# A two-layer block on one core: ends of stages by token halves, low parts in place, second layer by projection

## The chip, the core and the metric

The kernel runs on one core of one Trainium2 chip (trn2). The metric is the time of one execution on the device in microseconds (us). The program uses TensorE (PE in the profile, with its weight loads as PEld), VectorE (DVE), ScalarE (ACT), GpSimd (POOL) and SyncE (SP), which issues the loads and stores.

## The reference, cut to what matters

The input x is 256 tokens by 1024 channels in float32, with a context of 256 tokens and a conditioning vector. Two parts follow each other.

```python
# part 1, twice (a0, a1)
shift, scale, gate = split(silu(c) @ w_ada + b_ada)      # one vector of 1024 each
h = rms_norm(x, pre_g) * (1 + scale) + shift
q, k, v, g = split(h @ w_in)                             # two groups of 8 heads, 64 wide
y = concat(attention_a * silu(ga), attention_b * silu(gb)) @ w_out
x = x + gate * rms_norm(y, post_g)
# part 2: m00 (on x and on the context), m01, m02, m10, m11, m12, each of the form
h = rms_norm(x, g) * (1 + scale) + shift
x = x + gate * sublayer(h)     # m00, m02, m10, m12: 0.5 * gate * (silu(h Wa) * (h Wb)) W2, width 2816
                               # m01: neighbourhood attention and a gated scan; m11: spatial gating
out = rms_norm(x, g_final)
```

The shifts, scales and gates are themselves products of the conditioning vector with large matrices.

## The kernel before, in words

All weights stream once from HBM as tiles of 128x2x512 float32 (512 KB): 40 tiles for each of a0 and a1, 66 for each of m00, m02, m10 and m12, 36 for m01 and 48 for m11. SP issues them, with the 188 and more tiles of the modulation matrices between them, into a ring of 7 slots, and waits for the release of a slot before each issue (`sp_program`).

A float32 product is made of three products in fp32r. ACT copies a tile to its high part (`act_tick`, recorded at L227), DVE subtracts that from the tile for the low part (`dve_tick`, L230), and PE computes high by high, low by high and high by low (L221). There are four pairs of buffers for high and low parts (sb_sp0h, sb_sp0l and so on), so ACT is three tiles ahead at most. The activations lie transposed, split in the same way, in hTh and hTl. In the time order of DVE stand the products of modulation tiles with the conditioning vector too (`dve_vector`, CUSTOM_DVE_ANT_0 of 128x1024 at L241), which a table VT assigns to tiles; in a1 a tile has two of them, since each matrix tile serves two conditions.

There are two forms of matmul work on a tile. `pe_unit` keeps hT stationary and moves the weights, 512 columns, once per token half: 12 matmuls of N=512. `pe_up` (the first matrix of each FFN) keeps the weights stationary and moves the 256 tokens: 24 matmuls of N=256.

Every stage ends the same way. The last tile's matmuls run for both token halves. Then DVE multiplies the four banks with the gate (`dve_residual`) and adds them to X, ACT and DVE take the squares, DVE the mean, POOL the power -0.5 (`pool_rstd`), and DVE normalizes four pieces into XN (`dve_normalize`, L234). PE transposes them in 16 pieces (`pe_norm`, L224). ACT and DVE apply scale and shift, and ACT, DVE and POOL write the high and low parts (`act_norm`, `dve_norm`, `pool_norm`). Then comes the first matmul of the next stage. Each engine runs its instructions in the written order; semaphores tie them together. Nothing of this order comes from a scheduler.

In a0 and a1 (`pe_block1`) the attention of the heads is laid between the weight tiles by the table B1: heads of group A at units 14 to 24, of B at 25 to 31.

Of the kernel before, what the change touches and what calls it, by code (L numbers as in the profile page):

```python
# [79 lines left out]
def weight_tiles():  # L80


    out = []
# [81 lines left out]
AHEAD = 3  # L165


def stream_order():

    out = []  # L170
    for c in range(4):
        out += [("m", 4 * c + i) for i in range(4)] + [("w", 3 * c + i) for i in range(3)]
    for t in range(12 - AHEAD, W_ALL):
        if t + AHEAD < W_ALL:
            out.append(("w", t + AHEAD))
        out += [("m", n) for n in VT.get(t, ())]
    return out
# [105 lines left out]
def build(nc, I, out):  # L283
    ctx = ExitStack()
    with ctx:
# [86 lines left out]
        LD = {k: signal("load_" + k) for k in ("cb", "cb2", "cst", "vec", "x", "pos", "xc", "blk0", "blk1", "small", "mlm", "nb0", "nb1",  # L372
                                                "sg", "fg", "out")}
        slot_load = [signal(f"slot{i}") for i in range(NSLOT + NMORE)]


        more = [at_arena(f"wx{i}", 5888 + i * 1024, [128, 2, 512]) for i in range(NMORE)]
        ORDER = stream_order()
        SLOT, holder = {}, {}
        PREV = {}  # L380
        for n, item in enumerate(ORDER):
            s = n if n < NSLOT + NMORE else (n - NMORE) % NSLOT if n >= 2 * NSLOT + NMORE else n - NSLOT - NMORE
            PREV[item] = holder.get(s)
# [22 lines left out]
        def sp_program(e):  # L406
            e.dma(CB[0][:, :], I["cvec"][0:1, :].partition_broadcast(128)).then_inc(LD["cb"].sem, LD["cb"].put(0, by=16))
            e.dma(X[:, :, :], I["x"].rearrange("(j p) d -> p j d", p=128)).then_inc(LD["x"].sem, LD["x"].put("x", by=16))
            for n, item in enumerate(ORDER):
# [5 lines left out]
                if PREV[item] is not None:  # L415
                    e.wait_ge(*release(PREV[item]))
                s = slot_load[SLOT[item]]
                src = I["w" if item[0] == "w" else "mw"][item[1]].rearrange("p (k n) -> p k n", k=2)
                e.dma(ring[SLOT[item]][:, :, :], src).then_inc(s.sem, s.put(item, by=16))
            for j in range(2):  # L420
                e.wait_ge(*done(DE, "final", j))
                e.dma(out[j * 128:(j + 1) * 128, :], XN[:, j, :]).then_inc(LD["out"].sem, LD["out"].put(j, by=16))
            e.wait_ge(*done(LD["out"], 1))
# [14 lines left out]
        def dve_tick(e, t, ahead=AHEAD, vectors=True):  # L438

            while cursor["lo"] <= min(t + ahead, W_ALL - 1):  # L440
# [3 lines left out]
                h, l = SPL[n % 4]  # L444
                e.tt(l[:, :, :], ring[SLOT["w", n]][:, :, :], h[:, :, :].bitcast(F32), ALU.subtract).then_inc(LO.sem, LO.put(n))
# [90 lines left out]
        def square_dve(e, s, src, j, nh, after):  # L536
            for f in after:
                e.wait_ge(*f)
            c = slice(nh * 512, (nh + 1) * 512)
            e.ttr(XN[:, j, c], src[:, j, c], src[:, j, c], 1 / 1024, ALU.mult, ALU.add, ssq[:, NS[s], j, nh:nh + 1],  # L540
                  0.0).then_inc(DE.sem, DE.put("square", s, j, nh))
# [1678 lines left out]
```

## Time and profile before

| | us |
|---|---|
| median of 3 runs | 1785.08 (1783.41 to 1785.38) |
| profiled execution | 1780.99 |
| its span, first to last instruction | 1779.2 |
| PE busy | 1653.8 (93% of the span) |
| DVE busy | 1210.0 (68%) |
| ACT busy | 709.6 (40%) |
| POOL busy | 57.6 (3%) |

The mean granted TensorE clock is 0.969 of full speed. A busy PE is not a PE at its peak: the matmuls overlap, and how many are done in a time is seen from the distance of their starts, not from the length of one. The idle time before a stage's first transpose is the place where a stage's end shows.

### The profile page before, as it was taken

The page shows a single profiled execution, that of the slowest core. Times are in us where ns is not written, and L with a number is a line of the kernel's source. Part 1 is how long each engine was busy: PE and PEld are TensorE (multiplying, and loading weights), DVE is VectorE, ACT ScalarE, POOL GpSimd, SP SyncE. Part 2 cuts the span into 40 slices and gives each one's busy share as a digit, 9 for nine tenths or more (in the row PEclk, how much of TensorE's full clock was granted, in tenths as well). Part 3 has the DMA queues.
Part 4 walks back from the last instruction along what each step waited for, and adds up shares of the span by engine and source line. Part 5 has one row for each costly group of instructions (what it writes and reads, how often), then busy time and mean ns, then how long its engine had stood idle before and what let it go on. Part 6 is the DMA issues. An engine that isn't in the chain of part 4 may idle for free.

```text
span 1779.2 us, 23063 instructions
## 1 busy us (share of the span) xinstructions
PE 1653.8 (93%) x9138; PEld 1415.2 (80%) x9138; DVE 1210.0 (68%) x2088; ACT 709.6 (40%) x1026; POOL 57.6 (3%) x73
## 2 busy tenths in 40 slices
PE   4989887999999999979997999998999899989997
PEld 3766665778888888868775789987999788889986
DVE  6866797768996666465556677766776656665544
ACT  3455443553222222143344444444444355444442
POOL 1000100000000000020001000000000000000000
PEclk9989998899999999989998999999999999999999
DMA  9855494434785766333222257775877666345551
GB/s 354 298 182 187 154 331 152 154 119 144 237 292 193 244 231 221 129 99 107 83 71 66 76 203 263 253 239 178 277 253 252 229 224 202 118 165 181 184 181 71
DMA packets 92844, 338.04 MB, mean 190 GB/s; under 512 B 10608, under 2 KB 11120, under 8 KB 92480
## 3 DMA queue, kind: packets, MB, share of 16 engines
q1 hardware_dynamic: 90416, 328.11, 54.8%
q0 software_dynamic: 2320, 8.46, 1.4%
q8 instruction: 72, 1.18, 0.3%
q14 instruction: 36, 0.29, 0.1%
HBM read 335.47 MB, written 1.05 MB: 189 GB/s over the span
## 4 chain that ended last, share of the span: by engine, by line
PE 67%; issue 13%; DVE 12%; ACT 5%; DMA 1%; POOL 1%; SPq 0%; DVEq 0%; POOLq 0%; ACTq 0%
PE bank L221 64%; PE bank L224 3%; DVE sb_w L241 2%; ACT sb_arena L227 2%; DVE sb_tmw L241 1%; DVE sb_arena L241 1%; DVE sb_tm L230 1%; ACT sb_sp2h L227 1%; DVE sb_sg L235 1%; DVE sb_sp3l L230 1%; DVE sb_sp2l L230 1%; ACT sb_sg L227 1%; DMA sb_vec<-in_vecs 1%; DVE sb_hTh L248 1%; DVE sb_sp0l L230 1%
## 5 line engine op out<-in xcount | busy, mean ns | idle before, releaser
L230 DVE TENSOR_TENSOR sb_sp3l<-sb_w,sb_sp3h 128x1024 fp32r<-128x1024 f32 x106 | 130.6, 1232 | 110.9 <-ACT sb_sp3h L227 110.6
L230 DVE TENSOR_TENSOR sb_sp2l<-sb_w,sb_sp2h 128x1024 fp32r<-128x1024 f32 x107 | 131.2, 1226 | 98.4 <-ACT sb_sp2h L227 98.4
L230 DVE TENSOR_TENSOR sb_sp0l<-sb_w,sb_sp0h 128x1024 fp32r<-128x1024 f32 x106 | 129.7, 1223 | 96.2 <-ACT sb_sp0h L227 95.8
L230 DVE TENSOR_TENSOR sb_sp1l<-sb_w,sb_sp1h 128x1024 fp32r<-128x1024 f32 x106 | 130.3, 1229 | 91.3 <-ACT sb_sp1h L227 91.0
L227 ACT ACTIVATE sb_sp2h<-sb_w 128x1024 fp32r<-128x1024 f32 x107 | 113.1, 1057 | 175.4 <-PE bank L221 149.0
L227 ACT ACTIVATE sb_sp0h<-sb_w 128x1024 fp32r<-128x1024 f32 x106 | 112.1, 1057 | 175.4 <-PE bank L221 150.1
L241 DVE CUSTOM_DVE_ANT_0 sb_w<-sb_w,sb_cb 128x1024 f32<-128x1024 f32 x144 | 175.8, 1227 | 0.0
L227 ACT ACTIVATE sb_sp3h<-sb_w 128x1024 fp32r<-128x1024 f32 x106 | 112.0, 1057 | 139.0 <-PE bank L221 116.4
L227 ACT ACTIVATE sb_sp1h<-sb_w 128x1024 fp32r<-128x1024 f32 x106 | 112.0, 1056 | 130.5 <-PE bank L221 112.9
L221 PE MATMUL bank<-sb_hTh,sb_sp0h 128*128 128x256 f32 (+1 forms) x360 | 110.8, 308 | 1.7 <-DVE sb_sg L230 1.7
L221 PE MATMUL bank<-sb_hTh,sb_sp3l 128*128 128x256 f32 (+1 forms) x360 | 110.5, 307 | 0.5 <-DVE sb_sp3l L230 0.5
L221 PE MATMUL bank<-sb_hTl,sb_sp0h 128*128 128x256 f32 (+1 forms) x360 | 110.7, 307 | 0.1
L221 PE MATMUL bank<-sb_hTh,sb_sp2h 128*128 128x256 f32 (+1 forms) x360 | 110.7, 308 | 0.0
L221 PE MATMUL bank<-sb_hTl,sb_sp1h 128*128 128x256 f32 (+1 forms) x360 | 110.5, 307 | 0.2 <-POOL sb_hTl L230 0.2
L221 PE MATMUL bank<-sb_hTh,sb_sp0l 128*128 128x256 f32 (+1 forms) x360 | 110.6, 307 | 0.0
L221 PE MATMUL bank<-sb_hTl,sb_sp2h 128*128 128x256 f32 (+1 forms) x360 | 110.5, 307 | 0.0
L221 PE MATMUL bank<-sb_hTh,sb_sp2l 128*128 128x256 f32 (+1 forms) x360 | 110.4, 307 | 0.0
L221 PE MATMUL bank<-sb_hTh,sb_sp3h 128*128 128x256 f32 (+1 forms) x360 | 110.4, 307 | 0.0
L221 PE MATMUL bank<-sb_hTh,sb_sp1h 128*128 128x256 f32 (+1 forms) x360 | 110.3, 307 | 0.0
L221 PE MATMUL bank<-sb_hTl,sb_sp3h 128*128 128x256 f32 (+1 forms) x360 | 110.3, 307 | 0.0
L221 PE MATMUL bank<-sb_hTh,sb_sp1l 128*128 128x256 f32 (+1 forms) x360 | 110.3, 307 | 0.0
L221 PE MATMUL bank<-sb_arena 128*128 128x64 f32 (+5 forms) x400 | 89.7, 355 | 19.9 <-ACT sb_arena L227 11.5
(461 smaller groups left out, 4161.2 us busy)
## 6 DMA issues: line engine op xcount, KB each, us to landing
sb_w<-in_w SPq DMA_DIRECT2D x425, 512.0 KB, 4.2
sb_w<-in_mw SPq DMA_DIRECT2D x188, 512.0 KB, 4.5
sb_wx<-in_mw SPq DMA_DIRECT2D x4, 512.0 KB, 14.2
sb_wx<-in_w SPq DMA_DIRECT2D x3, 512.0 KB, 15.5
sb_G<-in_na_rpb POOLq DMA_DIRECT2D x16, 96.0 KB, 2.8
sb_X<-in_x SPq DMA_DIRECT2D x1, 1024.0 KB, 7.5
sb_cb<-in_cvec POOLq DMA_DIRECT2D x2, 512.0 KB, 9.0
sb_XC<-in_ctx POOLq DMA_DIRECT2D x1, 1024.0 KB, 5.9
```

Source lines behind the costliest of these rows:

```text
L221: return self.e.matmul(out, a, b, start=start, stop=stop)
L224: return self.e.transpose(out, a, ident)
L227: return self.e.activation(out, a, f, **kw)
L230: return self.e.tensor_tensor(out, a, b, op)
L235: return self.e.tensor_scalar(out, a, s1, s2, op0, op1, **kw)
L241: return self.e.tensor_tensor_reduce(out=out, in0=a, in1=b, scale=scale, scalar=init, op0=op0, op1=op1, accum_out=accum)
L248: return self.e.tensor_copy(out, a)
```

## The change

Five things change together.

1. **Token halves.** The last four tiles of a stage run for token half 0 and then for half 1. New functions `dve_edge`, `act_edge`, `pool_edge` (and `dve_edge1`, `act_edge1` in part 1) do residual, norm and split of one half while PE works on the other. The next stage's first four tiles ("head") run for half 0 and then for half 1, first the terms that need hTh ("hl"), then the one that needs hTl ("a"). In a1, m01 and m11 this is `pe_head`, with N=512 as before. In m00, m02, m10 and m12 it is `pe_up_head`, where the tokens are what moves, so each matmul has N=128 and there are twice as many.
2. **Buffers.** The low part overwrites the raw tile in its ring slot (`ring_r`), and the slot is released when PE has used the tile. There are 9 slots, with some more in regions that are free at times (`place_stream`), and six to eight buffers for high parts (`high_buffers`); a tile's high part waits for the release of the buffer's former tile (HPREV).
3. **Second layer.** a1 computes q, k and v one after the other, four tiles each, rather than interleaved. Its attention starts earlier: group A at units 11 to 21, B at 22 to 32. In a0 the heads of B are spread over units 25 to 33.
4. **Context.** In m00 the context's last product stays where it was, but its residual stands behind m01's `dve_edge`; the first three weight units of m01 are part of the head, so the small gate products follow directly on the context's norm.
5. **The end.** The last residual and the final norm go by token halves, with four output transfers of 256 KB.

The diff, cut to its core (the first lines are the new head and its call):

```diff
+        def pe_up_head(e, s, t0, key, banks, ns):
+
+            for j in range(2):
+                pe_norm(e, s, j)
+                for terms in ("hl", "a"):
+                    for k in range(4):
+                        pe_up(e, t0 + k, key, banks, ns, j * 128, 128, 2 * k, hT_ready(s), ns == 1 and j == 0 and terms == "hl",
+                              j == 1 and terms == "a", j == 1 and terms == "a", terms)
...
+        def pe_head(e, s, t0, key, banks, j0=0):
+            for j in range(2):
+                if j >= j0:
+                    pe_norm(e, s, j)
+                for terms in ("hl", "a"):
+                    for k in range(4):
+                        pe_unit(e, t0 + k, key, HPARTS, 2 * k, banks, (j,), hT_ready(s), k == 0 and terms == "hl",
+                                k == 3 and terms == "a", used=j == 1 and terms == "a", terms=terms)
...
-        def act_tick(e, t, ahead=AHEAD):
+        def act_tick(e, t, last=W_ALL - 1):
-            while cursor["hi"] <= min(t + ahead, W_ALL - 1):
+            while cursor["hi"] <= last and HPREV[cursor["hi"]] < t:
                 n = cursor["hi"]
                 cursor["hi"] += 1
                 e.wait_ge(*landed(("w", n)))
-                if n >= 4:
-                    e.wait_ge(*done(USED, n - 4))
-                e.act(SPL[n % 4][0][:, :, :], ring[SLOT["w", n]][:, :, :], ACT.Copy).then_inc(HI.sem, HI.put(n))
+                if HPREV[n] >= 0:
+                    e.wait_ge(*done(USED, HPREV[n]))
+                e.act(HI_[HB[n]][:, :, :], ring[SLOT["w", n]][:, :, :], ACT.Copy).then_inc(HI.sem, HI.put(n))
...
-                e.tt(l[:, :, :], ring[SLOT["w", n]][:, :, :], h[:, :, :].bitcast(F32), ALU.subtract).then_inc(LO.sem, LO.put(n))
+                e.tt(ring_r[s][:, :, :], ring[s][:, :, :], HI_[HB[n]][:, :, :].bitcast(F32), ALU.subtract).then_inc(
+                    LO.sem, LO.put(n))
...
+        def dve_edge(e, s, t0, residual, hfree):
+            residual(0)
+            dve_mean(e, s, 0, [done(SQ, s, 0, nh) for nh in range(2)])
+            if HPREV[t0 + 7] >= t0:
+                dve_tick(e, t0 + 2, vectors=False)
+            dve_normalize(e, s, 0, X)
+            dve_turned(e, s, 0, 1)
+            dve_high(e, s, 0, 0, hfree)
+            residual(1)
+            dve_turned(e, s, 0, 3)
+            dve_high(e, s, 0, 2, hfree)
+            dve_mean(e, s, 1, [done(SQ, s, 1, nh) for nh in range(2)])
+            dve_low(e, s, 0, 0)
+            dve_low(e, s, 0, 2)
+            dve_normalize(e, s, 1, X)
...
+            dve_tick(e, t0 + 4, vectors=False)
...
+            B1[1].setdefault(11 + i, []).append(("A", i))
+            B1[1].setdefault(22 + i, []).insert(0, ("B", i))
```

How the order on the engines changes is seen at three places. The first is PE at the start of m10. XN is the normalized X, sb_cst the identity for the transposes, sp0h and sp0l the split of the first tile; the last row is a matmul of the three terms that repeat.

```order
4860 L221 MATMUL bank<-sb_sp3h,sb_gTm020l 128x512
4861 L224 MATMUL bank<-sb_cst,sb_XN 128x128 x16
4862 L221 MATMUL bank<-sb_hTh,sb_sp0h 128x256
4863 L221 MATMUL bank<-sb_hTl,sb_sp0h 128x256
4864 L221 MATMUL bank<-sb_hTh,sb_sp0l 128x256
```

After the change the same place has 8 transposes, then the head for half 0 (hi_76 to hi_79 are high parts of four tiles, w1r a low part in its ring slot), and 8 more transposes behind it:

```order
4932 L271 MATMUL bank<-sb_hi_75,sb_gTm020l 128x512
4933 L274 MATMUL bank<-sb_cst,sb_XN 128x128 x8
4934 L271 MATMUL bank<-sb_hTh,sb_hi_76 128x128
4935 L271 MATMUL bank<-sb_hTh,sb_w1r 128x128
...
4998 L271 MATMUL bank<-sb_hTl,sb_hi_76 128x128 x8
4999 L271 MATMUL bank<-sb_hTl,sb_hi_77 128x128 x8
5000 L271 MATMUL bank<-sb_hTl,sb_hi_78 128x128 x8
5001 L271 MATMUL bank<-sb_hTl,sb_hi_79 128x128 x8
5002 L274 MATMUL bank<-sb_cst,sb_XN 128x128 x8
```

Between the two groups of transposes now stand 96 matmuls of N=128; the same count follows for half 1, where before there were 96 of N=256 in all.

The second place is DVE at the end of the mixer (m01 into m02), first before:

```order
1291 L230 TENSOR_TENSOR sb_sp0l<-sb_w_55,sb_sp0h 128x1024
1292 L230 TENSOR_TENSOR sb_tm_78<-bank,sb_G_72 128x512
1293 L230 TENSOR_TENSOR sb_X<-sb_X,sb_tm_78 128x512
1294 L230 TENSOR_TENSOR sb_tm_79<-bank,sb_G_72 128x512
1295 L230 TENSOR_TENSOR sb_X<-sb_X,sb_tm_79 128x512
1296 L241 ISA sb_XN,sb_ssq<-sb_X 128x512
1297 L241 ISA sb_ssq 128x1
1298 L238 SCALAR_TENSOR_TENSOR sb_rstd<-sb_ssq 128x2
1299 L234 TENSOR_SCALAR sb_XN<-sb_X,sb_rstd 128x512 x4
```

and the same place after the change:

```order
1289 L280 TENSOR_TENSOR sb_w8r<-sb_w_65,sb_hi_75 128x1024
1290 L280 TENSOR_TENSOR sb_tm_89<-bank,sb_G_83 128x512
1291 L280 TENSOR_TENSOR sb_X<-sb_X,sb_tm_89 128x512
1292 L280 TENSOR_TENSOR sb_tm_89<-bank,sb_G_83 128x512
1293 L280 TENSOR_TENSOR sb_X<-sb_X,sb_tm_89 128x512
1294 L288 SCALAR_TENSOR_TENSOR sb_rstd<-sb_ssq 128x1
1295 L280 TENSOR_TENSOR sb_w4r<-sb_w_57,sb_hi_76 128x1024
1296 L280 TENSOR_TENSOR sb_w1r<-sb_w_51,sb_hi_77 128x1024
1297 L280 TENSOR_TENSOR sb_w6r<-sb_w_61,sb_hi_78 128x1024
1298 L280 TENSOR_TENSOR sb_w3r<-sb_w_55,sb_hi_79 128x1024
1299 L284 TENSOR_SCALAR sb_XN<-sb_X,sb_rstd 128x512 x2
```

Four low parts of whole tiles (rows 1295 to 1298) now stand between the mean of half 0 and its normalization; this is the `dve_tick` in `dve_edge`, which only m01 and m02 have.

The third place is PE in m01 behind the context's norm. Before, weight units follow on its 16 transposes, and the gate products (72x256) come 24 matmuls later:

```order
2808 L221 MATMUL bank<-sb_sp3h,sb_hTl 128x512
2809 L224 MATMUL bank<-sb_cst,sb_XN 128x128 x16
2810 L221 MATMUL bank<-sb_sp0h,sb_hTh 128x512
2811 L221 MATMUL bank<-sb_sp0l,sb_hTh 128x512
2812 L221 MATMUL bank<-sb_sp0h,sb_hTl 128x512
```

After the change the gate products follow at once:

```order
2863 L271 MATMUL bank<-sb_hi_77,sb_hTl 128x512 x2
2864 L274 MATMUL bank<-sb_cst,sb_XN 128x128 x16
2865 L271 MATMUL bank<-sb_hTh,sb_gwh 72x256
2866 L271 MATMUL bank<-sb_hTl,sb_gwh 72x256
2867 L271 MATMUL bank<-sb_hTh,sb_gwl 72x256
```

The units that stood between them have moved ahead of the transposes, into the head.

## Rows read from the trace of the kernel before

**Rows 1.** The page's totals by engine: busy us, share of the span, instructions.
```profile
PE 1653.8 (93%) x9138; PEld 1415.2 (80%) x9138; DVE 1210.0 (68%) x2088; ACT 709.6 (40%) x1026; POOL 57.6 (3%) x73
```
**Rows 2.** Busy us inside m02, with count; then PEclk, DMA share, GB/s.
```profile
1040.00:1217.00 177.00, 177.00 (x1251) 166.73 (x1250) 125.63 (x154) 75.82 (x80) 0.00 (x0) 1.00 0.78 261
```
**Rows 3.** PE timeline, eight long waits: start, us, instruction, [idle before <-releaser].
```profile
120.26 1.11 PE L224 MATMUL bank<-sb_cst,sb_arena 128*128 128x128 f32 x4 [2.58 <-DVE sb_stat L241]
...
208.85 0.87 PE L224 MATMUL bank<-sb_cst,sb_XN 128*128 128x128 f32 x2 [7.50 <-DVE sb_XN L234]
...
262.24 1.61 PE L221 MATMUL bank<-sb_arena 64*128 64x128 f32 x4 [7.08 <-DVE sb_arena L248]
...
396.41 0.39 PE L221 MATMUL bank<-sb_hTh,sb_sp0h 128*128 128x256 f32 x1 [1.70 <-DVE sb_sg L230]
...
775.43 0.80 PE L221 MATMUL bank<-sb_sp2h,sb_hTh 128*128 128x512 f32 x1 [8.80 <-ACT sb_sp2h L227]
...
1027.30 1.09 PE L224 MATMUL bank<-sb_cst,sb_XN 128*128 128x128 f32 x3 [6.14 <-DVE sb_XN L234]
...
1423.15 1.21 PE L224 MATMUL bank<-sb_cst,sb_XN 128*128 128x128 f32 x4 [4.99 <-DVE sb_XN L234]
...
1577.39 0.87 PE L224 MATMUL bank<-sb_cst,sb_XN 128*128 128x128 f32 x2 [4.94 <-DVE sb_XN L234]
```
**Rows 4.** PE timeline at m10's start.
```profile
1225.24 3.77 PE L224 MATMUL bank<-sb_cst,sb_XN 128*128 128x128 f32 x16 [4.99 <-DVE sb_XN L234]
1228.66 0.56 PE L221 MATMUL bank<-sb_hTh,sb_sp0h 128*128 128x256 f32 x1
...
1231.94 0.28 PE L221 MATMUL bank<-sb_hTh,sb_sp1h 128*128 128x256 f32 x1
...
1234.82 0.28 PE L221 MATMUL bank<-sb_hTh,sb_sp2h 128*128 128x256 f32 x1
```
**Rows 5.** PE timeline in a0: transposes, and matmuls of 64 columns in float32.
```profile
173.20 0.49 PE L224 MATMUL bank<-sb_cst,sb_arena 128*128 128x128 f32 x3
173.53 0.78 PE L221 MATMUL bank<-sb_arena 128*128 128x64 f32 x6
174.14 0.50 PE L224 MATMUL bank<-sb_cst,sb_arena 128*128 128x128 f32 x3
175.13 1.52 PE L221 MATMUL bank<-sb_arena 128*128 128x64 f32 x12 [0.48 <-DVE sb_XN L234]
176.46 0.48 PE L221 MATMUL bank<-sb_sp0h,sb_yT0h 128*128 128x512 f32 x1
```
**Rows 6.** DVE timeline from m02's last low part to m10's normalization.
```profile
1218.69 1.23 DVE L230 TENSOR_TENSOR sb_sp2l<-sb_w,sb_sp2h 128x1024 fp32r<-128x1024 f32 x1 [1.52 <-ACT sb_sp2h L227]
1219.83 0.68 DVE L230 TENSOR_TENSOR sb_tm<-bank,sb_G 128x512 f32<-128x512 f32 x1
...
1223.63 0.16 DVE L238 SCALAR_TENSOR_TENSOR sb_rstd<-sb_ssq 128x2 f32<-128x2 f32 x1
1224.61 1.67 DVE L234 TENSOR_SCALAR sb_XN<-sb_X,sb_rstd 128x512 f32<-128x512 f32 x4 [0.81 <-POOL sb_rstd L230]
```
**Rows 7.** ACT timeline: a square at m02's end, m10's first turned rows.
```profile
1221.28 0.63 ACT L227 ACTIVATE sb_XN<-sb_X 128x512 f32<-128x512 f32 x1 [2.62 <-DVE sb_X L230]
...
1226.49 1.02 ACT L227 ACTIVATE sb_sg<-bank,sb_mods 128x256 f32<-128x256 f32 x2 [4.49 <-PE bank L224]
```
**Rows 8.** DVE timeline in a1: a tile's low part, two vectors, the next low part.
```profile
286.59 1.23 DVE L230 TENSOR_TENSOR sb_sp1l<-sb_w,sb_sp1h 128x1024 fp32r<-128x1024 f32 x1 [0.58 <-ACT sb_sp1h L227]
287.73 1.22 DVE L241 CUSTOM_DVE_ANT_0 sb_tmw<-sb_w,sb_cb 128x1024 f32<-128x1024 f32 x1
...
293.04 1.22 DVE L230 TENSOR_TENSOR sb_sp2l<-sb_w,sb_sp2h 128x1024 fp32r<-128x1024 f32 x1 [1.53 <-ACT sb_sp2h L227]
```
**Rows 9.** DVE timeline at the program's end.
```profile
1768.76 0.69 DVE L230 TENSOR_TENSOR sb_tm<-bank,sb_G 128x512 f32<-128x512 f32 x1 [7.24 <-PE bank L221]
...
1773.55 2.48 DVE L238 SCALAR_TENSOR_TENSOR sb_XN<-sb_X,sb_rstd,sb_PG 128x1024 f32<-128x1024 f32 x2 [0.82 <-POOL sb_rstd L230]
```

More of the change, by code:

```diff
@@ L625, in pool_norm @@
[L625 to L636 removed]
+                    dve_high(e, s, p, c2, hfree)
@@ L641, in hT_ready, with all_split, rows_turned @@
         def hT_ready(*stages):
-            return lambda kc, part: [h_ready(s, kc, part) for s in stages]
-        def pe_unit(e, t, key, parts, at, banks, cols, which, ready, first, last, used=True):
-            h, l = SPL[t % 4]
+            return lambda kc, part, xs: [h_ready(stages[x // 2], kc, part, x % 2) for x in xs]
+        def all_split(*stages):
+            return [f for s in stages for p in parts_of(s) for f in (done(DE, "hl", s, p, 2), done(PO, "hl", s, p, 3))]
+        def rows_turned(s):
+            return [done(TRP, "norm", s, p, 3) for p in parts_of(s)]
@@ L648, in pe_unit, with h_cols, cols_of @@
+        def h_cols(t):
+            return lambda kc, x: t[:, x // 2, kc, x % 2 * 128:x % 2 * 128 + 128]
+        def cols_of(t):
+            return lambda kc, x: t[:, kc, x * 128:x * 128 + 128]
+        HPARTS = h_cols(hTh), h_cols(hTl)
+        def pe_unit(e, t, key, parts, at, banks, which, ready, first, last, used=True, terms="hla"):
+            h, l = HI_[HB[t]], ring_r[SLOT["w", t]]
             ah, al = parts
@@ new lines, in dve_total, with dve_residual @@
+        def dve_total(e, dst, nh, j, till, tag):
+            c = slice(nh * 512, (nh + 1) * 512)
+            e.wait_ge(*done(DE, *till, j))
+            e.tt(dst[:, j, c], dst[:, j, c], TM[j][:, :], ALU.add).then_inc(RES.sem, RES.put(*tag, j, nh))
+        def dve_residual(e, dst, g, gate, banks, ends, nh, till, tag):
+            for j in range(2):
+                dve_gated(e, g, gate, banks[j], ends[j], nh, j, till)
+            for j in range(2):
+                dve_total(e, dst, nh, j, till, tag)
@@ L1413, in pe_mixer @@
             pe_context_tail(e)
-            pe_norm(e, "m01")
-            for u in range(36):
+            AB.i = 0
+            for u in range(32):
                 key, at, first, last = mx_tile(u)
@@ L1982, in pe_spatial @@
         def pe_spatial(e):
-            pe_norm(e, "m11")
-            for u in range(48):
+            AB.i = 0
+            for u in range(44):
                 key, at, first, last = sg_tile(u)
@@ L2027, in act_spatial @@
                         e.wait_ge(*done(DE, "ln_mean", j))
-                        e.wait_ge(*done(TRP, "norm", "m11", 3))
+                        for f in rows_turned("m11"):
+                            e.wait_ge(*f)
                         e.wait_ge(SQ, SQ.n)
```

878 lines of the change are left out of this document (518 added, 360 removed), and 4 rows, old and new, of the table B1.

## The prediction

> **What bounds the kernel now.** I read the totals by engine first [rows 1]: PE is busy for 93% of the span, DVE for 68%, ACT for 40%. So the time is PE's work plus PE's waits. The second view is busy time by stretch: inside m02, from 1040 to 1217 us, PE is busy for all 177.00 us at full clock, with DVE at 125.63 and ACT at 75.82 us [rows 2]. Within an FFN there is nothing to win by feeding PE better, and every matmul added there costs its whole interval. The third view is PE's timeline with its waits [rows 3, 4]. The stage ends are the large ones: 7.50 us ahead of a1, 1.70 ahead of m00, 8.80 (m01), 6.14 (m02), 4.99 (m10), 4.99 (m11), 4.94 (m12). A further 7.08 lies within a1 at 262 us.
>
> A wait costs more than its length. After the 4.99 us at m10, sixteen transposes take from 1225.24 to 1228.66, 3.42 us [rows 4], 0.214 each; three of them in a running stretch take from 173.20 to 173.53, 0.11 each [rows 5]. That is the lower of the two clock levels against the higher, and 3.42 - 16 x 0.11 = 1.7 us on top of the wait.
>
> At m10, then: wait 5.0, low clock 1.7, and about 0.3 on the first weight matmuls: 7.0 us between what PE did and what it could have done. Counted the same way the ends cost 8.6 (a1), 3.1 (m00), 12.6 (m01, with its context norm), 8.1 (m02), 7.0, 6.9 (m11), 6.7 (m12), and the tail 9.1, from PE's last end at about 1770.1 to the span's end at 1779.2. Together 62 us: the most that the change can take from the ends.
>
> **The cost: the heads of the FFNs.** In the four `pe_up_head`s 96 matmuls of N=256 become 192 of N=128; N=512 units gain no matmul by the split. The distance of N=256 is read from a tile: 24 of them from 1231.94 to 1234.82, 0.12 each [rows 4]. No row has fp32r at N=128, so I bound it. Below: half, 0.12 / 2 plus nothing, say 0.067 if the 0.013 over the 0.107 that 256 columns take at 2.4 GHz stays. Above: a matmul of 512 columns, 0.23, if a short one were to be worked through in four passes. The nearest row is the one with small matmuls in float32: 12 of 64 columns between 175.13 and 176.46, 0.111 each, and 6 between 173.53 and 174.14, 0.102 each [rows 5]. These stream few columns and still keep the distance of a transpose. Nothing in the trace with its own stationary operand runs closer than 0.10. In the head each matmul has a new stationary operand of 128 columns too. I take 0.11: a head costs 192 x 0.11 = 21.1 us where it cost 96 x 0.12 = 11.5, so 9.6 more, four times: **+38.4 us**. The bounds: +1.3 x 4 = +5 at 0.067, and (192 x 0.23 - 11.5) x 4 = +131 at 0.23.
>
> The Trainium skill, in TensorE: Matmul & The Clock Gate, section LDWEIGHTS (loading the stationary operand), gives a weight load as its columns over 1.2 GHz, about 107 ns for 128 columns; the 0.111 and 0.102 us of [rows 5] agree with that. By the section Back-to-back issue gap of the same page a stream at N=128 is sustained at about 81 ns a matmul; by that a head would cost 192 x 0.081 = 15.6 us and the four +16 us, which speaks for less cost than I take and belongs to rival C below. No run here shows it.
>
> **What the ends give back.** At m10 the new chain for half 0 starts when its banks end, with half 1 of the last four tiles still to run: 4 x 6 matmuls of 512 columns at 0.23, 5.5 us. The chain: product and sum 0.72 + 0.73, a square 0.63 and its readout (about 0.7), mean to normalize 0.98 with the power on POOL, two of the four pieces 0.84 [rows 6, 7]: 4.0 us, hidden. What stays is 8 transposes and scale, shift and cast of the first rows, some 1.5 us that nothing hides. Half 1's chain (residual, norm, split, 8 to 9 us of DVE) lies under 96 matmuls, 10.6 us. So 7.0 becomes 1.5, **-5.5**. The same way m12 -5.2, and m11, whose head of N=512 is short beside its chain, -4.7. No wait of over 2 us is left there, so no low clock.
>
> m02: between mean and normalization stand four low parts, 1.14 us from start to start (1218.69 to 1219.83, [rows 6]), so 4.6 us on the chain that has 5.5 to hide in: 8.1 becomes about 6.0, **-2.1**. m00: only the split of half 0 is waited for, **-1.6**. a1: both halves' squares come before the first normalization, and two low parts stand in the chain: **+1**, bounds -7 and +2.
>
> m01 is the stage where waits are added. The tick in its edge needs the release of a tile by the context's third product, ahead of which DVE and ACT can do nothing for the half: PE waits 2.9 us at the first transposes. The context's residual now stands on DVE behind the whole edge, and PE comes to the context's transposes after a head of 4 x 12 x 0.23 = 11 us: a wait of about 4.9. The gate products, once hidden behind 24 matmuls, stand right behind those transposes and wait for their split: about 4.5. With the low clock after each (1.7) the worst sum is 17.4 against 12.6. If the edge runs smoothly it is 4. I take 15.6, nearer to the first since each wait is in the written order: **+3**, bounds +5 and -8.5.
>
> The tail: one half's product, sums, norm and output are done under the other's matmuls. The last chain has one piece of 512 where two of 1024 columns took 2.48 us [rows 9], but the same chain of readout, mean and power: **-1.7**.
>
> Part 1: in a0 the four waits between 89 and 122 us, of which the last is 2.58 [rows 3], sum to 7.4; heads of B spread wider give some of them back: **-3**. In a1 the 7.08 at 262 us goes, since q, k and v of the first heads are there four to eight tiles earlier. But the attention now runs in more units together with two vectors each. Such a unit takes 293.04 - 286.59 = 6.45 us of DVE [rows 8] against 21 x 0.23 = 4.8 of PE. Three more units of that pair, 1.65 each, and a gap in its place: **-1**, bounds -9 and +7.
>
> Buffers, ring and stores I cost at nothing: within a stage PE waits for no transfer, with DMA at 0.78 of its time [rows 2], and two more slots can only help; if the later release of a slot (at use, not at the low part) bites, it costs some us in a1 and m00.
>
> **The sum.** -5.5 - 5.2 - 4.7 - 2.1 - 1.6 + 1 + 3 - 1.7 - 3 - 1 = -20.8, and +38.4: +17.6 us. The profiled execution took 1781.0 us; 1781.0 + 17.6 = 1798.6. The median of the runs is 4.1 above that execution, so the forecast is 1802.7, rounded to 1803, slower by 1%.
>
> **Rivals.** Mechanism C, on the other side: a matmul of 128 columns costs half of one of 256. Then the heads cost 5 us, the sum is -16 and the time 1769. For it: 512 and 256 columns cost in proportion, 0.23 and 0.12. Against it: [rows 5]. It decides from (46.1 + 20.8) / 768 = 0.087 us a matmul, where 46.1 us is what the four heads had before, 384 x 0.12: anywhere below, the kernel is faster.
>
> The 81 ns of the Trainium skill (TensorE: Matmul & The Clock Gate, Back-to-back issue gap) lie on this side: 768 x 0.081 - 46.1 - 20.8 = -5, a time of 1780.
>
> Mechanism D: the short matmuls cost far more than 0.11, either since fp32r is only fast from 256 columns on, or since the granted clock falls in a stretch where PE mostly loads weights; the low clock's row is 0.214 each [rows 4], four passes 0.23. Then a head takes 41 to 44 us, four cost +118 to +131, and the time is 1785 + 125 - 21 = 1889. For it: no row shows fp32r below 256. Against it: transposes and the float32 matmuls of 64 columns hold 0.11 at the high clock.
>
> Mechanism B: 0.11 holds, and the ends give nothing back, since DVE with its extra small instructions is late for the heads and the waits only move: 1785 + 38 = 1823. For it: m01's three waits; against it: the slack of 5.5 and 10.6 us at m10.
>
> That the change doesn't do what it says would be a head that waits for hTl's half 1 before its first matmuls; the written order rules it out.
>
> **Chances.** My forecast 0.57, with its own range 1790 to 1815; B 0.12; C 0.15; D 0.16. A measurement of this kernel tells a change from none at about 0.2%, 3.6 us. Faster: C's 0.14 and 0.07 of mine, where m01, a1 and a0 all come out at their good ends: 0.21. Same: 0.07, nearly all of it mine too. Slower: 0.72, with the rest of mine, B and D. The range leaves out D and holds the rest: 1762 to 1830.
>
> **What would show it.** The start distance of the 128-column matmuls in m02, m10 and m12: 0.11 right, 0.067 C, over 0.2 D. The waits ahead of m10, m11, m12: under 2 us each, with the eight transposes at 0.11. At m02 four subtractions between mean and normalization and a wait of 3 to 5 us. At m01 three waits. If the head takes 21 us and the time still falls, the ends or a1 held more than I read from them.

## The result and the profile after

The changed kernel takes 1854.01 us (median of 4 runs, 1851.72 to 1861.19) against 1785.23 us before in the same comparison: a ratio of 1.0394, 95% interval 1.0364 to 1.0423. The direction was forecast; the time was not: it lies 51 us above the forecast of 1803 and 24 above the upper end of the range, 1830. The profiled execution has a span of 1849.8 us, 70.6 more than before. The totals of the page after answer to [rows 1]:

```profile
PE 1723.0 (93%) x9522; PEld 1476.6 (80%) x9522; DVE 1205.5 (65%) x2104; ACT 719.4 (39%) x1080; POOL 63.9 (3%) x96
```

PE is busy 69.2 us longer, nearly all of the 70.6: its idle time is 126.8 us against 125.4 before. So the waits as a whole have moved, not grown, and what grew is the time in which PE works, by more instructions and by a lower clock. To find where, I measured each stage from its first transpose to the next one's, in both traces:

| stretch, from first transposes to first transposes | before | after | difference |
|---|---|---|---|
| start to a1 | 192.2 | 190.3 | -1.9 |
| a1 to the context's norm | 171.4 | 182.7 | +11.3 |
| context's norm to m00's | 27.8 | 33.9 | +6.1 |
| m00's norm to the context's norm in m01 | 376.7 | 403.0 | +26.3 |
| rest of m01, to m02 | 242.6 | 237.6 | -4.9 |
| m02 to m10 | 197.9 | 224.4 | +26.5 |
| m10 to m11 | 197.9 | 202.3 | +4.4 |
| m11 to m12 | 154.2 | 149.5 | -4.7 |
| m12 to the end | 201.8 | 209.4 | +7.6 |

Where a stage begins with N=512 and no look-ahead is at stake (m11) it gets shorter; the FFNs m10 and m12 get 4 to 8 us longer; two stretches grow by 26 us each. The first stretch varies from run to run: in the seven later profiles that leave a0 as changed it takes 185.4 to 188.6 us instead of 190.3, and with a0 as before it is 195.3 in a second profile instead of 192.2. So its -1.9 is no measure of a0. The row of a1 is firm: 182.2 to 183.4 us in six later profiles that leave it as changed.

Next, PE's timeline at the places of [rows 3]:

```profile
206.98 1.09 PE L274 MATMUL bank<-sb_cst,sb_XN 128*128 128x128 f32 x8 [1.44 <-DVE sb_XN L284]
...
218.53 0.69 PE L274 MATMUL bank<-sb_cst,sb_XN 128*128 128x128 f32 x2 [2.98 <-DVE sb_XN L284]
...
252.95 1.97 PE L274 MATMUL bank<-sb_cst,sb_arena 128*128 128x128 f32 x8 [6.23 <-DVE sb_arena L280]
...
262.30 1.28 PE L271 MATMUL bank<-sb_arena 64*128 64x128 f32 x4 [4.15 <-DVE sb_arena L298]
...
407.91 0.58 PE L271 MATMUL bank<-sb_hTh,sb_hi 128*128 128x256 f32 x1 [3.92 <-DVE sb_tm L280]
...
412.46 0.58 PE L271 MATMUL bank<-sb_hTh,sb_hi 128*128 128x256 f32 x1 [2.89 <-DVE sb_tm L280]
...
573.09 0.76 PE L271 MATMUL bank<-sb_hi,sb_gTm000h 128*128 128x512 f32 x1 [8.85 <-ACT sb_sg L277]
...
803.29 0.41 PE L274 MATMUL bank<-sb_cst,sb_XN 128*128 128x128 f32 x2 [2.96 <-DVE sb_XN L284]
...
826.53 0.87 PE L274 MATMUL bank<-sb_cst,sb_XN 128*128 128x128 f32 x2 [4.04 <-DVE sb_XN L284]
...
1064.14 1.38 PE L274 MATMUL bank<-sb_cst,sb_XN 128*128 128x128 f32 x8 [2.78 <-DVE sb_XN L284]
1066.74 0.44 PE L271 MATMUL bank<-sb_hTh,sb_hi 128*128 128x128 f32 x1 [1.22 <-DVE sb_tm L280]
```

The 7.50 us ahead of a1 have become 1.44 and 2.98, the 8.80 of m01 2.96 and 4.04, the 6.14 of m02 2.78 and 1.22. The 7.08 within a1 has not gone, as forecast, but become 6.23 and 4.15, ahead of the first heads. Two places of waiting are new: 3.92 and 2.89 ahead of m00, and 8.85 in the middle of m00, where [rows 3] had none. At m10 the same view shows no wait at all before the transposes and 0.68 us before the head:

```profile
1288.32 0.40 PE L271 MATMUL bank<-sb_hi,sb_gTm020l 128*128 128x512 f32 x1
1288.56 1.04 PE L274 MATMUL bank<-sb_cst,sb_XN 128*128 128x128 f32 x8
1290.27 0.30 PE L271 MATMUL bank<-sb_hTh,sb_hi 128*128 128x128 f32 x1 [0.68 <-DVE sb_hTh L298]
1290.41 0.28 PE L271 MATMUL bank<-sb_hTh,sb_w1r 128*128 128x128 f32 x1
```

The price of the short matmuls is read from stretches that hold nothing else. Columns: stretch, its length, busy (count) of PE, PEld, DVE, ACT and POOL, granted clock, DMA share, GB/s. First the two halves of m02's head, then those of m10's:

```profile
1066.80:1087.20 20.40, 20.40 (x96) 20.40 (x96) 4.96 (x11) 1.78 (x5) 1.37 (x3) 0.50 0.08 30
1089.40:1109.80 20.40, 20.40 (x96) 20.40 (x97) 8.62 (x12) 5.16 (x8) 1.59 (x2) 0.50 0.17 64
1290.30:1301.00 10.70, 10.70 (x96) 10.70 (x97) 4.37 (x10) 1.83 (x6) 2.09 (x3) 1.00 0.19 75
1302.70:1313.40 10.70, 10.70 (x96) 10.70 (x97) 9.03 (x13) 7.34 (x11) 1.60 (x2) 1.00 0.13 39
```

At the higher clock 96 of them take 10.8 us from the first start to what follows, 0.112 each, as taken. In m02 the granted clock is 0.50 for the whole head, 43 us long with its transposes, and each takes 0.214. The weight loads (PEld) keep their unit busy throughout in all four. The head over, matmuls of 256 columns follow, and the clock is back after about 3 us:

```profile
1110.00:1114.00 4.00, 4.00 (x25) 4.00 (x25) 2.54 (x5) 3.72 (x4) 0.00 (x0) 0.68 1.01 386
1114.00:1120.00 6.00, 6.00 (x52) 6.00 (x51) 5.39 (x7) 2.12 (x2) 0.00 (x0) 1.00 0.98 380
```

The cause of the 8.85 us in m00 is read on ACT, in the timeline of the same stretch:

```profile
567.29 1.06 ACT L277 ACTIVATE sb_hi<-sb_w 128x1024 fp32r<-128x1024 f32 x1 [2.45 <-DMA sb_w<-in_w]
571.40 1.06 ACT L277 ACTIVATE sb_hi<-sb_w 128x1024 fp32r<-128x1024 f32 x1 [3.06 <-DMA sb_w<-in_w]
572.37 1.06 ACT L277 ACTIVATE sb_sg<-bank 128x512 f32<-128x512 f32 x2
```

ACT stands for 2.45 and then for 3.06 us at the copies of tiles that have not landed. The silu (sb_sg), whose end releases the waiting matmul, is behind them in the order and starts the moment the second copy is through.

### The profile page after: what moved, and what is told of

It reads as the page before. It is cut to its first block and busy times, and to the rows that moved or that the text cites. A ratio compares the mean times of both kernels' runs of the same rounds, so it can differ in the third digit from the quotient of the medians.

```text
span 1849.8 us, 23930 instructions
## 1 busy us (share of the span) xinstructions
PE 1723.0 (93%) x9522; PEld 1476.6 (80%) x9522; DVE 1205.5 (65%) x2104; ACT 719.4 (39%) x1080; POOL 63.9 (3%) x96
## 5 line engine op out<-in xcount | busy, mean ns | idle before, releaser
L277 ACT ACTIVATE sb_hi<-sb_w 128x1024 fp32r<-128x1024 f32 x428 | 447.6, 1056 | 624.9 <-PE bank L271 453.2
L271 PE MATMUL bank<-sb_hTh,sb_hi 128*128 128x256 f32 (+2 forms) x1568 | 478.0, 311 | 12.1 <-DVE sb_tm L280 8.0
L271 PE MATMUL bank<-sb_hTl,sb_hi 128*128 128x256 f32 (+2 forms) x1568 | 443.4, 310 | 0.0
L271 PEld LDWEIGHTS bank<-sb_hTh,sb_hi 128*128 128x128 f32 x1568 | 309.2, 197 | 28.4 <-DVE sb_tm L280 7.3
L271 PEld LDWEIGHTS bank<-sb_hTl,sb_hi 128*128 128x128 f32 x1568 | 286.9, 197 | 12.5
L271 PE MATMUL bank<-sb_hi,sb_hTh 128*128 128x512 f32 x560 | 232.5, 415 | 10.8 <-DVE sb_hTh L298 8.0
L271 PE MATMUL bank<-sb_hi,sb_hTl 128*128 128x512 f32 x560 | 217.7, 401 | 0.6 <-POOL sb_hTl L280 0.6
L271 PEld LDWEIGHTS bank<-sb_hi,sb_hTh 128*128 128x128 f32 x560 | 110.0, 196 | 40.8 <-issue 16.5
L271 PEld LDWEIGHTS bank<-sb_hi,sb_hTl 128*128 128x128 f32 x560 | 109.3, 195 | 25.8 <-POOL sb_hTl L280 1.2
L271 PEld LDWEIGHTS bank<-sb_arena 128*128 128x128 f32 (+1 forms) x400 | 56.8, 197 | 45.7 <-issue 27.2
```

The lines of the kernel that those rows point to most:

```text
L271: return self.e.matmul(out, a, b, start=start, stop=stop)
L277: return self.e.activation(out, a, f, **kw)
```

## The experiments

Each is an edit of the changed kernel unless said otherwise, and its time stands beside runs of the kernel before on the same chip. Single runs of kernels with short heads differ by up to 28 us, so the stage in the profile decides, not the median.

**Two low parts instead of four at m02**

```diff
             if HPREV[t0 + 7] >= t0:
-                dve_tick(e, t0 + 2, vectors=False)
+                dve_tick(e, t0 + 2, t0 + 7, vectors=False)
```

> The changed kernel with two low parts (and high copies) instead of four between the mean and the normalization at the end of the mixer; the other two follow at the end of the edge. Theory A (a 128-column stream does not bring the clock back once a wait has dropped it): the 2.78 us wait ahead of m02 shrinks to about 0.5 us, the clock stays at 1.00, each half of the head takes 10.8 instead of 20.5 us, the time falls by 20 to 24 us to about 1832. Rival B (the low clock in m02's head has another cause at that place): only the 2.3 us of the two low parts go, about 1851.

Measured: 1857.76 us (2 runs), ratio 1.0389 (1.0313 to 1.0465). The first wait shrinks as expected, the clock does not stay. PE's timeline at m02's head:

```profile
1064.40 1.09 PE L274 MATMUL bank<-sb_cst,sb_XN 128*128 128x128 f32 x8 [0.51 <-DVE sb_XN L284]
1067.01 0.30 PE L271 MATMUL bank<-sb_hTh,sb_hi 128*128 128x128 f32 x1 [1.51 <-DVE sb_tm L280]
1067.14 0.32 PE L271 MATMUL bank<-sb_hTh,sb_w5r 128*128 128x128 f32 x1
1067.26 0.42 PE L271 MATMUL bank<-sb_hTh,sb_hi 128*128 128x128 f32 x1
```

The first matmul runs at full clock (0.30), the third no longer (0.42). Now the clock falls inside the head, and stays at 0.50 for both halves. So the number is rival B's: nothing of the 20 us came back. Theory A's price for a low clock holds, its trigger (the 2.78 us) does not: here the clock falls behind waits of 0.51 and 1.51 us.

**A wait added at m10**

```diff
+            if s == "m10":
+                for i in range(6):
+                    ...
+                    e.tt(TM[0][:, :], TM[0][:, :], TM[0][:, :], ALU.mult).then_inc(DE.sem, DE.put("more", s, i))
             dve_normalize(e, s, 0, X)
```

> The changed kernel with six idle multiplications of 128x512 (about 0.7 us each) on DVE between mean and normalization of m10's half 0, a stage whose head ran at full clock. Theory A: PE waits about 3 us ahead of m10's transposes, the granted clock is 0.50 until the head is over, the head takes 41 instead of 21.5 us: 23 us more, about 1877. Rival B (only m02 is affected): 3 us of wait and 1.7 us of slow transposes, about 1859.

Measured: 1884.97 us in the profiled run and 1856.81 in the other; the two differ by more than the 20 us of one head's clock, and no ratio is given. In the profile PE waits 1.88 us at m10, and its head runs at half clock; m12's, with no wait ahead of its transposes, does not. PE's timeline, then the stretches of m10's two halves, of the wide matmuls behind them and of m12's first half:

```profile
1300.36 1.48 PE L274 MATMUL bank<-sb_cst,sb_XN 128*128 128x128 f32 x8 [1.88 <-DVE sb_XN L284]
1302.10 0.45 PE L271 MATMUL bank<-sb_hTh,sb_hi 128*128 128x128 f32 x1 [0.26 <-DVE sb_hTh L298]
```

```profile
1303.00:1322.00 19.00, 19.00 (x91) 19.00 (x91) 3.52 (x9) 1.06 (x3) 1.37 (x3) 0.50 0.00 1
1325.00:1345.00 20.00, 20.00 (x95) 20.00 (x96) 10.49 (x13) 7.96 (x11) 1.58 (x2) 0.50 0.18 55
1350.00:1360.00 10.00, 10.00 (x86) 10.00 (x84) 6.77 (x9) 4.79 (x5) 0.00 (x0) 1.00 0.64 215
1676.00:1686.00 10.00, 10.00 (x92) 10.00 (x92) 3.81 (x10) 1.28 (x4) 1.69 (x3) 1.00 0.13 52
```

So m02 is no special place: a short head behind a wait of 2 us can run low at m10 too, and costs 20 us then (m10's interval is 1524.21 - 1300.36 = 223.9 against 202.3). It need not. The other run, 1856.81 us, is rival B's number and leaves no room for 20 us more than in the changed kernel; it has no profile, so what its m10 did is not shown. Theory A's price holds again; that the wait always brings the low clock is not shown.

**Short heads in the kernel before**

```diff
                         for k in range(4):
-                            pe_up(..., ns, 0, 256, 2 * k, hT_ready(s), False, True, True)
+                            for j in range(2):
+                                pe_up(..., ns, j * 128, 128, 2 * k, hT_ready(s), False, j == 1, j == 1)
```

(and the same for the three FFNs on x alone)

> The kernel before, with nothing changed but the first four tiles of m00, m02, m10 and m12, whose matmuls on x go in two of 128 columns each. Theory A: m00's enters at full clock and costs 192 x 0.112 - 11.5 = 10 us; m02, m10 and m12 enter at half clock after their waits of 5 to 6 us and stay there, 192 x 0.214 - 11.5 = 30 us each: +100 us, about 1885. Rival B: 10 us each, +40, about 1825.

Measured: 1824.53 us, ratio 1.0203 (1.0164 to 1.0243), rival B's number: 35 us above the 1789.52 of the kernel before beside it. By stages, the four stretches that hold the heads grow by 9.3 (m00), 10.1 (m02), 10.2 (m10) and 10.1 us (m12), 39.7 together. PE's timeline at m10:

```profile
1249.35 3.77 PE L224 MATMUL bank<-sb_cst,sb_XN 128*128 128x128 f32 x16 [4.99 <-DVE sb_XN L234]
1252.77 0.45 PE L221 MATMUL bank<-sb_hTh,sb_sp0h 128*128 128x128 f32 x1
...
1253.88 0.36 PE L221 MATMUL bank<-sb_hTh,sb_sp0l 128*128 128x128 f32 x1
1254.08 0.27 PE L221 MATMUL bank<-sb_hTh,sb_sp0h 128*128 128x128 f32 x1
```

Here the clock comes back after 1.1 us of short matmuls. What went before them differs: sixteen transposes on end, with no wait behind them, where the changed kernel has eight and a wait of 1.2 us. This run settles the heads' term of the sum: 192 short matmuls cost 10 us more than 96 wide ones, four times, when the clock is up. And it refutes theory A as I had put it, that a short stream never sees the clock return.

**Heads of 256 columns in the changed kernel**

```diff
             for j in range(2):
                 pe_norm(e, s, j)
-                for terms in ("hl", "a"): ... j * 128, 128 ...
+            for k in range(4):
+                pe_up(e, t0 + k, key, banks, ns, 0, 256, 2 * k, hT_ready(s), ns == 1, True, True)
```

> The changed kernel with both halves' transposes ahead of the FFN heads and the heads in matmuls of 256 columns again; all else as changed. Theory A with the sizes of the trace: 38 us of short matmuls and 20 us of low clock in m02 go; PE now waits for half 1's chain in four places, 5 to 7 us each with the slow clock after it: 1854 - 58 + 25 = about 1821. Rival C (the halves hide nothing, their chains are as short as the head is long): no wait comes back, about 1796.

Measured: 1830.48 us, ratio 1.0237 (1.0192 to 1.0282), 9 above theory A's number. Half 1's chain is now in the open: 7.03 us at m00, 6.54 at m02, 4.94 at m10 and m12. PE's timeline at m10, and the stretch behind:

```profile
1269.12 1.04 PE L274 MATMUL bank<-sb_cst,sb_XN 128*128 128x128 f32 x8
1275.10 1.94 PE L274 MATMUL bank<-sb_cst,sb_XN 128*128 128x128 f32 x8 [4.94 <-DVE sb_XN L284]
```

```profile
1276.00:1284.00 8.00, 6.78 (x30) 6.11 (x29) 7.45 (x12) 5.80 (x10) 1.59 (x2) 0.50 0.01 2
1284.00:1290.00 6.00, 6.00 (x51) 6.00 (x51) 4.21 (x6) 2.12 (x2) 0.00 (x0) 0.97 0.52 175
```

At m10 the wide head with its wait costs as much as the short one with none: the interval to m11 is 201.0 us against 202.3. Wide matmuls bring the clock back, in 7 us; the wait of m02 costs 22 us less (202.4 against 224.4). Rival C is out.

**More transposes at m02**

```diff
-                        m = e.tr(...)
+                        for _ in range(3 if (s, p) == ("m02", 0) else 1):
+                            m = e.tr(...)
```

The sixteen added transposes do nothing but fill PE.

> The changed kernel with each of the eight transposes of half 0 ahead of m02's head done three times over into the same place, 16 idle transposes more. Theory A2 (a stream of 128-column matmuls leaves the clock where it is, only a denser stretch such as transposes or 256 columns raises it): the added work costs 16 x 0.214 = 3.4 us at most, the clock is back when the head begins, the head takes 21.5 instead of 41 us, and the kernel is about 15 us faster than the changed one, 1839. Rival B (the head itself lowers the clock in that place): 3 us slower, 1857.

Measured: 1836.67 us, ratio 1.0284 (1.0254 to 1.0314): 17 us less than the changed kernel, with more work in it. PE's timeline and the first half of the head:

```profile
1070.43 2.84 PE L274 MATMUL bank<-sb_cst,sb_XN 128*128 128x128 f32 x24 [2.78 <-DVE sb_XN L284]
1073.86 0.30 PE L271 MATMUL bank<-sb_hTh,sb_hi 128*128 128x128 f32 x1 [0.59 <-DVE sb_tm L280]
```

```profile
1075.00:1084.00 9.00, 9.00 (x83) 9.00 (x83) 4.04 (x10) 1.35 (x5) 1.36 (x2) 1.00 0.02 8
```

The wait is the same 2.78 us. The transposes run at 0.11 each. So the clock was not raised again, which is what I had expected; it never fell. The interval to m10 is 204.1 us, 20.3 less. The number came in by a path that I had half wrong.

**Four high buffers inside m00, and then two more slots**

```diff
         free = [b for b in range(NHI + NHX) if ...]
+        if 92 <= n < 138:
+            free = free[:4]
```

The second kernel has this and eleven slots in the ring of tiles instead of nine, the two added ones for tiles 96 to 130.

> The changed kernel with four instead of six buffers for high parts for the tiles 92 to 137 inside m00, so that ACT's copies and DVE's subtractions stand three instead of five tiles ahead in the order, as before the change; still 9 slots. Theory L (ACT stands at the copy of a tile that has not landed, with the silu that PE needs queued behind it): the wait of 8.85 us in m00 goes, 8 to 12 us faster, 1843. Theory S (too few slots in the ring, each now held until PE has used the tile): no gain or some us slower, 1854 to 1858.

> As the run with four high buffers inside m00, and the two buffers set free there serve as two more ring slots for the weight tiles 96 to 130 (11 slots). Theory S: the wait of 8.85 us in m00 goes here and not with four buffers alone, 8 to 12 us faster than the changed kernel, 1843. Theory L: the same gain as with four buffers alone, nothing on top.

Measured: 1846.63 us (ratio 1.0340, 1.0235 to 1.0445) and 1849.32 us (1.0355, 1.0320 to 1.0390). By the totals that is unclear; by the stage it is not. The interval from m00's transposes to m01's is 379.7 us in the changed kernel, 372.6 with four buffers and 372.8 with four buffers and eleven slots. The wait of 8.85 us, which is 7.3 to 11.0 us in the five other profiles with m00's buffers as changed, is gone in both; one of 3.98 us, for a low part, appears at 510 us. Slots add nothing: theory S is out, and 7 us come back, a little under the 8 to 12 of theory L. One thing is not separated: the order in which SP issues the loads is sorted by the same table of buffers, so the edit also gives other places in it to 106 of the 620 loads. The trace shows silu behind late copies in the changed kernel; whether the copies' place or the loads' order gives back the 7 us is not shown.

**Late attention in a1**

```diff
-            B1[1].setdefault(11 + i, []).append(("A", i))
-            B1[1].setdefault(22 + i, []).insert(0, ("B", i))
+        B1[1] = {u: list(z) for u, z in B1[0].items()}   # and the context's entries at 34 and 35
```

> The changed kernel with a1's attention laid as in a0: first transposes at units 12 and 13, heads of group A at units 14 to 24, of B at 25 to 33; q, k and v still by projection. Theory D (the early attention meets DVE at its fullest, with two vectors a tile, and that is a1's loss of 11.6 us): the waits of 6.2 and 4.2 us at 253 and 262 us shrink and a1 gets 5 to 10 us shorter, about 1846. Rival E (a1's loss is the ring that starts empty after the head): no change within 3 us, 1854.

Measured: 1850.74 us, ratio 1.0363 (1.0251 to 1.0475); a1 takes 184.9 us instead of 182.7. The two waits have become one of 14.31:

```profile
272.02 0.77 PE L271 MATMUL bank<-sb_arena 64*128 64x128 f32 x2 [14.31 <-DVE sb_arena L298]
```

Theory D falls: the early attention does not cost a1 its 11 us, it saves some 2 (182.2 to 183.4 us in all profiles that have it with the changed buffers).

**Four high buffers in part 1 too**

```diff
+        if 20 <= n < 36 or 48 <= n < 76 or 92 <= n < 138:
+            free = free[:4]
```

> The changed kernel with four buffers for high parts for the tiles 20 to 35 of a0, 48 to 75 of a1 and 92 to 137 of m00 (before: six to eight), so that copies stand three tiles ahead in the order there. Theory L (copies of tiles that have not landed, placed five to seven tiles ahead, hold up what stands behind them on ACT) says that a1, whose attention's exponentials and copies stand behind them, gets 5 to 10 us shorter too, and m00 7 as before: about 1840. Rival D2 (a1 loses by its order of projections and attention, with DVE full): a1 unchanged within 2 us, about 1847.

Measured: 1835.66 us, ratio 1.0280 (1.0250 to 1.0309). a1 takes 177.4 us, 5.3 less; m00 takes 366.6 us, 13.1 less, with the same edit inside m00 that gave 7 before: the 3.98 us of that run are not there either (a single 1.67 stays). The wait of 6.23 us for the first heads' operands is 1.41 now:

```profile
243.98 1.10 PE L276 MATMUL bank<-sb_cst,sb_arena 128*128 128x128 f32 x8 [1.41 <-DVE sb_arena L282]
```

Rival D2 is out, and theory L stands, with the order of the loads (182 of 620 in other places here) not separated from the copies' place.

**The repairs together**

The edits of the two low parts, the transposes and the four buffers, and at the end of a1, on ACT and DVE, m00's first tiles ahead of the sums:

```diff
-            rows(0)
             if l == 1:
                 act_tick(e, W_B1[l] + 38)
+            rows(0)
...
-            total(0)
-            gated(1, 0)
             if l == 1:
                 dve_tick(e, W_B1[l] + 38, vectors=False)
+            total(0)
+            gated(1, 0)
```

> The changed kernel with all repairs that left its plan as it is: four high buffers inside a0, a1 and m00; at the end of a1 the copies and low parts of m00's head ahead of half 0's sums; two low parts instead of four at m02, and sixteen idle transposes there that bring the clock back. By the single runs: 17 us from m02's clock, 7 from m00, and the waits of 3.9 and 2.9 us ahead of m00 with the slow clock behind them, 8 in all: 1854 - 32 = about 1822, still 37 us above the kernel before, of which 38 are the short matmuls. Rival: the repairs share one cause (PE's idle time moves on) and give less than 20 us together, above 1834.

Measured: 1815.75 us, ratio 1.0168 (1.0086 to 1.0250); 1809.62 and 1821.88 in its two runs; the rival, above 1834, is out. Putting m00's low parts ahead of the sums gave only 2.2 us (31.7 against 33.9): of the two waits ahead of m00, 3.92 and 2.89 us, the second is 0.62 now and the first still 3.71. m02's first half ran at full clock, and the second shows the clock most plainly. PE's timeline:

```profile
1060.93 0.33 PE L273 MATMUL bank<-sb_hTh,sb_hi 128*128 128x128 f32 x1 [0.59 <-DVE sb_hTh L300]
1061.09 0.27 PE L273 MATMUL bank<-sb_hTh,sb_w1r 128*128 128x128 f32 x1
...
1063.43 0.28 PE L273 MATMUL bank<-sb_hTh,sb_hi 128*128 128x128 f32 x1
1063.55 0.38 PE L273 MATMUL bank<-sb_hTh,sb_w8r 128*128 128x128 f32 x1
1063.72 0.42 PE L273 MATMUL bank<-sb_hTh,sb_hi 128*128 128x128 f32 x1
```

After 0.59 us of wait and 2.6 us of short matmuls without a gap the clock falls, and the half takes 18 us. The same order of waits and matmuls at m10 and m12 keeps it.

**The buffers of before**

```diff
-NHI, NHX, ... = 6, 2, ...      NSLOT, NARENA, NCTX, NXC = 9, 7, 2, 2
+NHI, NHX, ... = 4, 0, ...      NSLOT, NARENA, NCTX, NXC = 7, 7, 0, 0
-            return (USED, USED.of(item[1])) if item[0] == "w" ...
+            return (LO, LO.of(item[1])) if item[0] == "w" ...
```

with the low parts in four buffers of their own and heads of 256 columns.

> The kernel with token halves and heads of 256 columns, with the buffers of before: 7 slots, released at the low part, four pairs for high and low parts, copies three tiles ahead, and the ticks that would otherwise block placed ahead of half 1's rows. Against the run with heads of 256 columns and the new buffers (1830): theory R (buffers and look-ahead cost a1 and m00 some 20 us together) says 1830 - 20 and some 5 us back at m01 and m02, where tail and head tiles now share four pairs: about 1815. Rival O (a1's and m00's losses come from the order of the work, not from the buffers): 1830 or above.

Measured: 1822.35 us, ratio 1.0205 (1.0175 to 1.0235), 8 less than the wide heads with the new buffers. From m00's transposes to m01's it is 365.7 against 378.1 us: 12.3 less. a1 gains nothing net, 182.4 against 183.4, since with four pairs its head waits 5.32 us for a copy and 4.67 for a low part. So theory R holds for m00 and only in part for a1, and the price on the other side is real: with four pairs the waits ahead of half 1's transposes are 8.87, 7.28 and 7.26 us at m02, m10 and m12, where they were 6.54, 4.94 and 4.94.

**Wide heads with the order of the edges mended**

On DVE half 1's sums, mean and normalization stand ahead of half 0's split, or of its later part, at m02, m10, m12 and m00; ACT and POOL to match; the transposes are not repeated; the rest as in the repairs. The order for m02, m10 and m12:

```diff
             dve_normalize(e, s, 0, X)
+            residual(1)
             dve_turned(e, s, 0, 1)
             dve_high(e, s, 0, 0, hfree)
-            residual(1)
+            dve_mean(e, s, 1, [done(SQ, s, 1, nh) for nh in range(2)])
+            dve_low(e, s, 0, 0)
+            dve_normalize(e, s, 1, X)
             dve_turned(e, s, 0, 3)
             dve_high(e, s, 0, 2, hfree)
-            dve_mean(e, s, 1, [done(SQ, s, 1, nh) for nh in range(2)])
-            dve_low(e, s, 0, 0)
             dve_low(e, s, 0, 2)
-            dve_normalize(e, s, 1, X)
```

> The repairs of the run before (without the idle transposes), and the four FFN heads in matmuls of 256 columns behind both halves' transposes, with half 1's sums, squares, mean and normalization put ahead of half 0's splitting on DVE, ACT and POOL. Token halves stay in a1, m01 and m11 with their 512 columns, and at the end. From the stages of the run before (1816): m02, m10, m12 and m00 lose their short matmuls, 10 us each and 18 in m02, together 48, and get back waits of about 3 us and some slow clock, 4 x 3 to 4 x 5: 1816 - 48 + 16 = about 1784, no difference from before that is clear; 1776 if the waits stay under 2 us. Rival: the order of the edges is not what bounds half 1 and the waits of 5 to 7 us of the first run with wide heads stay: 1795.

Measured in 6 runs: 1793.92 us, ratio 1.0048 (1.0036 to 1.0061). The waits are 3.41 us at m10 and m12, as expected, and 5.16 at m02. The number is the rival's 1795, 10 us above the forecast, though the waits at m10 and m12 did shrink from 4.94 to 3.41; so the mechanism is right and the sum is not. PE's timeline at m10:

```profile
1237.38 1.03 PE L276 MATMUL bank<-sb_cst,sb_XN 128*128 128x128 f32 x8
1241.83 1.64 PE L276 MATMUL bank<-sb_cst,sb_XN 128*128 128x128 f32 x8 [3.41 <-DVE sb_XN L286]
```

It is 60 us faster than the changed kernel and still 0.5% slower than before; its runs lie within 4 us of each other. m10 takes 198.8 us against 197.9 before, m11 149.5 against 154.2; a1 is 5.5 us above before, the stretch from the context's norm to m00 4.1, and the one from m00's transposes to m01's 5.6 (362.24 against 356.68).

## Why the prediction was wrong, point by point

**Right: the price of a short matmul at full clock.** 0.11 was taken from transposes and 64-column matmuls [rows 5]; 0.112 was measured, and the four heads put into the kernel before cost +39.7 us by their stretches, against +38.4. Mechanism C is out: 0.112 lies well above its 0.067, and above the 0.081 that gave 1780.

**Right: the ends at m10, m11, m12 and the tail.** m11's interval fell by 4.7 us (forecast for m12's end -5.2). m10's rose by 4.4, of which 10 are its head: -5.6 for m11's end (forecast -4.7). From PE's last end to the span's end it is 6.9 us against 9.1, -2.2 (forecast -1.7). The steps of half 0's chain at m10 add up to 4.6 us, not to the 4.0 that I wrote; it still fits under the 5.5. m01 was judged too gloomily: its waits are 2.96, 4.04 and 0.7 us where I had 2.9, 4.9 and 4.5.

**The step that failed first: "so 9.6 more, four times".** I priced all four heads at the higher clock. "No wait of over 2 us is left there, so no low clock" held for m10, m11 and m12, for which it was written. At m02 I forecast a wait of 3 to 5 us, allowed no more for the low clock behind it than the 1.7 us of the other ends ([rows 4], where matmuls of 256 columns follow the transposes), and did not ask what the head of short ones would do at the lower clock. It stayed there for all of it: 41 us instead of 21.5, **+20**. The forecast even had the figure 0.214, in rival D, but as a condition on the whole stream, to be had everywhere or nowhere.

**The step that failed second: "Buffers, ring and stores I cost at nothing".** I looked for slots and transfers, found no wait for either, and missed what more high buffers do to the written order: ACT copies five to seven tiles ahead, and what PE needs soon stands behind a copy that waits for a far tile. Going back to four buffers gave 7.1, 6.9, 13.1 and 11.0 us in m00 in the four kernels with short heads that do so, and 5.3 in a1. That is **+7 to +13** in m00 and **+5** in a1 for the buffers, with the order of the loads in it.

**m00's entry and a1.** m00's entry was forecast at -1.6 and came out at +6.1. PE waits 3.92 and 2.89 us there, each time until DVE has read a bank (sb_tm), with a slow clock in between. The second of these reads stands on DVE behind the two low parts of m00's head (from 407.77 us); with those moved ahead of the sums the second wait shrank to 0.62, the first stayed at 3.71, and 2.2 us came back. Of a1's +11.3, 5.3 are the buffers, and 2.98 are the wait ahead of half 1's transposes at 218.53, which lies in this stretch, where the 7.50 of before lay ahead of it. The rest, about 3 us, is open: late attention is not it, and the old buffers only exchange it for other waits.

The sum: 1803 + 20 + 13 + 5 + 8 (m00's entry) + 7 (a1's rest, against -1) - 3 (m01 and the mixer) = 1853, with 1854 measured. It closes so well in part by the choice of 13 for m00, the largest of the four figures; with 7 it is 1847.

## What to carry to other kernels

In this kernel, splitting a stage's first matmuls into token halves cost nothing where the weights move (m11: -4.7 us), and 10 us per four tiles where the tokens move, more than the stall that it hides (m10: +4.4 in all). When buffers for looking ahead are added, count what stands behind each copy on its engine. Ahead of a stream of short matmuls, keep PE filled: here sixteen idle transposes saved 20 us in one kernel; in the kernel with all repairs they did so for the first half of the head, and the clock fell in the second.

## What the runs showed of the hardware that I had not expected

- A stream of fp32r matmuls of 128 columns, without a gap in it, runs at either clock level and can be left at the lower one: 0.214 us each for 41 us, against 0.112. In the profiled runs m02's head ran low throughout six times after small waits (0.5 to 2.8 us in front of the transposes, 1.0 to 1.5 behind them), once in its first half alone, behind the same waits, and once for most of its second. m12's never did, with 0.68 and 0.59 us; m10's did once, with 1.88.
- It can also fall within such a stream, 2.6 us after a wait of 0.59 us, and come back 1.1 us into one, when sixteen transposes at a stretch went before. With matmuls of 256 columns behind a slow stretch it came back each time, in 3 to 7 us. What decides between two equal-looking heads is not shown here.
- Six of the ten kernels with short heads vary from run to run by 9 to 28 us (1838.92 and 1854.34 for one of them, with the mean granted clock at 0.966 and 0.956), the other four by 2 to 4; the kernel before varies by 6.5 us in 11 runs, and the three with wide heads by 1 to 4.
